# Output projection of a hybrid decoder trunk: a weight slice, three statistics steps and the softmax merge take other places in the order

## The reference

```python
h    = rms_norm(x) * (1 + scale) + shift             # scale, shift, gate = silu(c) @ w_ada + b_ada
proj = h @ w_in                                      # split among groups A, B, C
A = mla_attention(...)                               # prompt: causal; samples: 32 cached pages each
B = rwkv7_time_mix(...)                              # recurrence, then a norm over each head of 64:
      on = (o - mean(o)) * rsqrt(var(o) + 64e-5) * g + b + bonus
C = chunk_gmlp(...)
mixed = concat(silu(gA) * A, silu(gB) * B, silu(gC) * C)   # 1032 tokens x 1024
x = x + gate * rms_norm(mixed @ w_out)
```

## Time and profile before

| | us |
|---|---|
| median of 3 runs | 1941.46 |
| the profiled execution, its own time | 1939.73 |
| its span, first to last instruction | 1938.0 |
| PE busy in the span | 1833.1 |
| DVE busy | 894.3 |
| ACT busy | 512.0 |

### The profile page before, as it was taken

How to read it: one execution, slowest core, us unless ns; L and a number is a source line. 1 busy time by engine, 2 the same in 40 slices (tenths; PEclk the granted TensorE clock), 3 DMA queues, 4 the chain that set the end, 5 groups by cost and what they waited for, 6 DMA issues and landing times. The chain is left out here.

```text
span 1938.0 us, 45850 instructions
## 1 busy us (share of the span) xinstructions
PE 1833.1 (95%) x19344; PEld 1141.3 (59%) x19344; DVE 894.3 (46%) x1985; ACT 512.0 (26%) x1186; POOL 181.6 (9%) x175
## 2 busy tenths in 40 slices
PE   3999999999999899999969999999999989999998
PEld 2565666666665566654436656766666656666543
DVE  2125124223495678765230340332325857777642
ACT  3111122223331333432221110222224223343221
POOL 0010000002330300000000200000023321000000
PEclk9999999999999999999989999999999999999999
DMA  9600000000023666643155000010001147665441
GB/s 376 249 12 28 22 22 22 22 22 22 23 68 100 190 202 195 191 173 147 69 203 208 1 28 22 22 33 22 11 22 39 52 131 209 193 203 149 187 167 41
DMA packets 105543, 198.66 MB, mean 103 GB/s; under 512 B 17410, under 2 KB 87580, under 8 KB 101620
## 3 DMA queue, kind: packets, MB, share of 16 engines
q1 hardware_dynamic: 105332, 195.67, 30.6%
HBM read 182.81 MB, written 21.26 MB: 105 GB/s over the span
## 5 line engine op out<-in xcount | busy, mean ns | idle before, releaser
L825 PE MATMUL PB<-RB,R 128*128 128x344 f32 x1632 | 493.2, 455 | 0.0
L825 PEld LDWEIGHTS PB<-RB,R 128*128 128x128 f32 x1632 | 302.0, 190 | 156.4 <-issue 15.2
L1689 PE MATMUL PB<-WUQ,Q 32*32 32x256 f32 x5120 | 199.0, 385 | 20.1 <-DVE WUQ L1870 12.0
L2074 PE MATMUL PB<-RB,R 128*128 128x512 f32 x496 | 214.9, 593 | 0.0
L1870 DVE STREAM_TRANSPOSE WUQ<-RB 128x512 f32<-128x512 f32 x316 | 203.4, 680 | 17.8 <-DMA RB<-in_cache 14.2
L2074 PEld LDWEIGHTS PB<-RB,R 128*128 128x128 f32 x496 | 93.9, 190 | 115.9 <-issue 113.8
L985 ACT ACTIVATE R<-PB 128x344 f32<-128x344 f32 x90 | 41.3, 458 | 401.8 <-PE PB L825 401.8
L1240 DVE TENSOR_TENSOR PB<-PB,CST 128x128 f32<-128x128 f32 x64 | 18.8, 295 | 222.0 <-PE PB L845 222.0
L1689 PEld LDWEIGHTS PB<-WUQ,Q 32*32 32x32 f32 x5120 | 90.0, 104 | 43.9 <-issue 27.7
L673 PE MATMUL PB<-RB,R 128*128 128x344 f32 x288 | 85.4, 460 | 1.8 <-PEq L250 1.8
L1122 DVE COPY R<-PB 128x320 f32<-128x320 f32 x16 | 7.9, 492 | 146.7 <-PE PB L684 146.7
(11 more groups left out here) (367 smaller groups left out, 2617.5 us busy)
## 6 DMA issues: line engine op xcount, KB each, us to landing
RB<-in_cache SPq DMA_DIRECT2D x512, 160.0 KB, 2.6
R<-in_w_in SPq DMA_DIRECT2D x44, 512.0 KB, 3.8
R<-in_w_ada SPq DMA_DIRECT2D x14, 1536.0 KB, 9.7
RB<-in_w_ada SPq DMA_DIRECT2D x6, 1536.0 KB, 16.6
RB<-out_x_stream SPq DMA_DIRECT2D x2, 4096.0 KB
out_x_stream<-RB SPq DMA_DIRECT2D x16, 512.0 KB
RB<-in_x_prompt SPq DMA_DIRECT2D x1, 4096.0 KB
RB<-in_w_out SPq DMA_DIRECT2D x8, 512.0 KB, 3.8
```

The lines of the kernel that those rows point to most:

```text
L825: mm = pe.matmul(jobbank(j)[:, 0:CH], ring[:, blkno[n] % 4, k, :], hT[:, k, chunk(c)], start=(k == 0), stop=(k == KT - 1))
L1689: mm = pe.matmul(PB[qp[o], 2 * (h % 2) + q % 2, 0:256], Q4[qp[q], g, :], k[qp[q], c], start=(g == 0), stop=(g == NB - 1), skip_group_check ...
L2074: mm = pe.matmul(PB[0:n, 2 * (t % 2) + hf, :], mixT[:, k, cols(t)], wo[:, k, hf * 512:(hf + 1) * 512], start=(k == 0), stop=(k == 5))
```

## The change

`w_out` slice 2 is loaded at the end of the attention block instead of at the start of the output block, and a third `WP` multiplies by it. In the attention block's lists the items of the end are put in another order on PE and DVE, and `FC` uses PSUM bank 4 instead of 5 and waits for `pp_done` 16 (the copy of the last `PT`) instead of `ty_done` 8. In the output block `mean(4)`, `mean(5)`, `var(4)`, `var(5)` come earlier on PE, tile 2 is one call of `project`, `square(4)` and `square(5)` come ahead of `sums(0)` on ACT, and on DVE `centre(4)`, `centre(5)` and `leave(0)` come ahead of `finish(2)` and `finish(3)`.

```diff
-PE_PLAN = PE_PLAN[:4] + [(0, "GT", 0)] + PE_PLAN[4:-1] + [wp(0)] + rec("Z0") + PE_PLAN[-1:] + rec("U0") + [fc(1), (NH - 1, "PT", 0)] + \
-    rec("H0") + [fc(2)] + rec("Z1") + [pv(0), pv(1)] + rec("U1") + [pv(2), fc(4)] + rec("H1") + [pv(3)] + rec("OO") + [fc(6), wp(1)]
+PE_PLAN = PE_PLAN[:4] + [(0, "GT", 0)] + PE_PLAN[4:-1] + rec("Z0") + PE_PLAN[-1:] + [wp(0)] + rec("U0") + [(NH - 1, "PT", 0), fc(1)] + \
+    rec("H0") + [fc(2)] + rec("Z1") + [pv(0), pv(1)] + rec("U1") + [fc(4), pv(2), pv(3)] + rec("H1") + [wp(1)] + rec("OO") + [fc(6), wp(2)]
...
-DVE_PLAN = pair_plan(DVE_PAIR) + [fc(1), fc(2)] + rec("H0") + [fc(3)] + rec("G0") + [fc(4)] + rec("H1") + [fc(5), fc(6)]
+DVE_PLAN = pair_plan(DVE_PAIR) + [fc(1)] + rec("H0", "G0") + [fc(2), fc(3), fc(4)] + rec("H1") + [fc(5), fc(6)]
...
     sp.dma_start(wuv2, dram("w_uv")).then_inc(s_uv, 16)
+    sp.wait_ge(kt_used, NB * NH)
+    sp.dma_start(wo[:, 2], dram("w_out")[:, 2]).then_inc(s_wo[2], 16)
...
 elif what == "FC":
-    pe.wait_ge(ty_done, NS)
+    pe.wait_ge(pp_done, NH)
     if g == 1:
         pe.wait_ge(cb_done, 1)
-        pe.transpose(PB[0:1, 5, 0:P], m1, ident).then_inc(cb_full, 1)
+        pe.transpose(PB[0:1, 4, 0:P], m1, ident).then_inc(cb_full, 1)
...
-    for k in (2, 3):
-        sp.dma_start(wo[:, k], dram("w_out")[:, k]).then_inc(s_wo[k], 16)
+    sp.dma_start(wo[:, 3], dram("w_out")[:, 3]).then_inc(s_wo[3], 16)
...
-    project(0, [2, 3])
+    project(0, [3])
     var(2)
     var(3)
     project(0, [6, 7])
     project(1, [0, 1, 2, 3])
     project(0, [4, 5])
-    project(1, [6, 7, 4, 5])
     mean(4)
     mean(5)
-    project(2, [0, 1, 2, 3, 6, 7])
+    project(1, [6, 7])
     var(4)
     var(5)
-    project(2, [4, 5])
-    for t in ORD[3:]:
+    project(1, [4, 5])
+    for t in ORD[2:]:
...
     for u in (2, 3):
         root(u)
+    for u in (4, 5):
+        square(u)
     for i, t in enumerate(ORD):
...
         if i == 1:
-            for u in (4, 5):
-                square(u)
             for u in (4, 5):
                 root(u)
...
     variance(3)
+    centre(4)
+    centre(5)
+    leave(0)
     finish(2)
     finish(3)
-    leave(0)
     for i in range(1, 9):
...
         leave(ORD[i])
         if i == 1:
-            centre(4)
-            centre(5)
             variance(4)
```

More of the change, by code:

```diff
@@ L1728, in _ @@
                         elif what == "FC":
-                            pe.wait_ge(ty_done, NS)
+                            pe.wait_ge(pp_done, NH)
                             if g == 1:
                                 pe.wait_ge(cb_done, 1)
-                                pe.transpose(PB[0:1, 5, 0:P], m1, ident).then_inc(cb_full, 1)
+                                pe.transpose(PB[0:1, 4, 0:P], m1, ident).then_inc(cb_full, 1)
                             elif g == 2:
                                 pe.wait_ge(cb_done, 2)
-                                pe.matmul(PB[:, 5, 256:257], g128, ones[0:1, 0:1], start=True, stop=True, skip_group_check=True).then_inc(cb_full, 1)
+                                pe.matmul(PB[:, 4, 256:257], g128, ones[0:1, 0:1], start=True, stop=True, skip_group_check=True).then_inc(cb_full, 1)
                             elif g == 4:
@@ L1739, in _ @@
                                 pe.wait_ge(cb_done, 4)
-                                pe.matmul(PB[:, 5, 258:259], gsum, gl, start=True, stop=True, skip_group_check=True).then_inc(cb_full, 1)
+                                pe.matmul(PB[:, 4, 258:259], gsum, gl, start=True, stop=True, skip_group_check=True).then_inc(cb_full, 1)
                             elif g == 6:
@@ L1743, in _ @@
                                 for r in range(2):
-                                    mm = pe.matmul(PB[:, 5, r * 32:(r + 1) * 32], osb[:, r * P:(r + 1) * P], gsum[:, 0:32], start=True, stop=True, skip_group_check=True)
+                                    mm = pe.matmul(PB[:, 4, r * 32:(r + 1) * 32], osb[:, r * P:(r + 1) * P], gsum[:, 0:32], start=True, stop=True, skip_group_check=True)
                                 mm.then_inc(os_full, 1)
@@ L1956, in _ @@
                             dve.wait_ge(cb_full, 1)
-                            dve.tensor_reduce(gm1, PB[0:1, 5, 0:P].rearrange("p (c m) -> p m c", c=4), AX.X, ALU.max)
+                            dve.tensor_reduce(gm1, PB[0:1, 4, 0:P].rearrange("p (c m) -> p m c", c=4), AX.X, ALU.max)
                             dve.drain()
@@ L1961, in _ @@
                             dve.wait_ge(cb_full, 2)
-                            dve.tensor_scalar(nM, PB[:, 5, 256:257], -SCALE, None, ALU.mult).then_inc(cb_done, 1)
+                            dve.tensor_scalar(nM, PB[:, 4, 256:257], -SCALE, None, ALU.mult).then_inc(cb_done, 1)
                         elif what == "FC" and g == 4:
@@ L1974, in _ @@
                             dve.wait_ge(cb_full, 3)
-                            dve.reciprocal(rw, PB[:, 5, 258:259])
+                            dve.reciprocal(rw, PB[:, 4, 258:259])
                             dve.drain()
@@ L1988, in _ @@
                             dve.wait_ge(os_full, 1)
-                            dve.tensor_copy(olat[:].rearrange("p r h b -> p r b h"), PB[:, 5, 0:64].rearrange("p (r b h) -> p r b h", r=2, h=H))
+                            dve.tensor_copy(olat[:].rearrange("p r h b -> p r b h"), PB[:, 4, 0:64].rearrange("p (r b h) -> p r b h", r=2, h=H))
             pf_in = sem("pf_in")
```

## The result

The kernel after takes 1971.83 us (median of 4 runs, 1970.85 to 1985.81), the kernel before on the same chip 1944.09 (4 runs, 1939.73 to 1948.31). The ratio is 1.0152, interval 1.0128 to 1.0177: slower, as forecast. Times the 1941.46 that the prediction started from, that is +29.5 us to 1971.0, where 23.4 had been forecast, and the median is 0.8 us above the end of the range. The profiled execution took 1974.9 us, with a span of 1973.2.

A forecast was written before the change was run, and what follows sets the result against it. PE, busy 95% of the span, was taken as the bound. Per layer 2.8 (attention gaps) + 6.9 (tile 2) + 2.0 (half clock) = 11.7, twice 23.4: 1963.1 from the profiled execution, 1964.9 from the median, said 1964; range 1955 to 1971.

The forecast's parts named there:

- attention gaps, new less old: From the last scores to the output block: PE gaps of 4.4 us in, 1.6 out, +2.8 a layer.
- `WP` 2 in, slice out: `WP` 2 adds 1.9 us in the attention block, two `project` matmuls leave the output block, 1.7: nothing, or +0.2.
- tile 2's wait: Output block: PE stands still 6.9 us a layer at tile 2's first matmul, until DVE's `finish(3)` is over.
- half clock behind tile 2's wait: Output block: PE's work after the 6.9 us gap runs at half clock for a while, costing 2.0 us a layer.
- half clock in the tail: Between the scores' end and the output block: the three gaps of 1.0 to 1.7 us cost no half clock.
- The bound of the kernel: Whole kernel: PE bounds it, busy 95% of the span; idle time added there moves everything behind it.
- The end of the attention block: New PE gaps of 1.0 at `Z`, 1.7 at `FC` 1, 1.7 at `FC` 2; old 0.70, 0.36, 0.52 go.
- The output block: DVE idles 8 us before `mean(4)`, so `finish(3)` ends late and PE waits 6.9 us a layer at tile 2.
- B + 39.2: Output block, us counted from its start B: when DVE ends `finish(3)`; PE is free for tile 2 at B + 32.3.
- The moved slice and its load: `w_out` slice 2's early load lands in 3.8 us, long before `WP` 2: costs nothing; the moved work nothing, or +0.2.
- TensorE's clock: Half clock follows the 6.9 us gap at tile 2, 2.0 us a layer; the attention block's shorter gaps pay nothing.
- The rival that named the tail's half clock: Clock falls in the attention block's end too: another 1.7 us a layer, 1966.5, 1968 from the median; chance 0.15.

The follow-up runs named there:

- fill attention: Kernel after, with two unread matmuls of 384 columns on PE ahead of each of `FC` 1 and `FC` 2; ratio to before 1.0090.
- fill output: Kernel after, with seven unread matmuls of 512 columns on PE ahead of tile 2 in the output block; ratio to before 1.0131.
- Merge back: Kernel after with `FC` 1's place on PE, DVE's attention list, `FC`'s bank and wait as before, `WP` places kept; ratio to before 1.0081.
- finish first: Kernel after, with DVE's `finish(2)` and `finish(3)` put back ahead of `centre(4)`, `centre(5)` and `leave(0)`; ratio to before 1.0055.
- tile 2 split: Kernel after, with PE's `project` of tile 2 in two calls, slices 0 to 3, 6, 7, then 4, 5; ratio to before 1.0047.
- fill one gap: Kernel after, with two unread matmuls of 384 columns ahead of `FC` 1 alone; one execution, tails 19.85 and 21.23 us.

## Why the prediction was right in its direction and short in its size

Forecast and measurement of each term, both layers together. The tail without half clock is that of fill attention, 19.84 and 19.85, with 1.93 for `WP` 2 where it stands alone. The output block without it is before's, less the moved slice, plus the wait: 134.20 - 1.72 + 6.72 = 139.20, and 134.94 likewise; fill output's 139.03 and 135.14 agree within 0.2.

| term | forecast | measured | from |
|---|---|---|---|
| attention gaps, new less old | 5.6 | 5.2 | 2 x (19.85 - 15.30 - 1.93) |
| `WP` 2 in, slice out | 0 | 0.4 | 2 x (1.93 - 1.72) |
| tile 2's wait | 13.8 | 13.4 | the waits of PE |
| half clock behind tile 2's wait | 4.0 | 5.1 | (141.13 - 139.20) + (138.11 - 134.94) |
| half clock in the tail | 0 | 5.5 | (21.89 - 19.84) + (23.32 - 19.85) |
| sum | 23.4 | 29.7 | of the unrounded terms |

*The bound of the kernel*, PE without slack from tile 2 on: right. The delay of each stage came out whole at the end of its layer: 13.5 us in layer 1 and 16.2 in layer 2, where the forecast was 11.7 a layer.
*The end of the attention block*: right to 0.1 us in each of three gaps, in who ends them, and in the old gaps that went. Merge back shows that the merge steps' places and wait make the two of them ahead of `FC` 1 and 2.
*The output block*: right, down to DVE's idle time (8 forecast, 8.59) and B + 39.2 (39.1). One step on the way was misread: two `square` were put at 1.6, where the earlier trace rows has 1.07 for the two, and the 0.4 taken off for overlaps made up for most of it. That B + 39.2 is so near is in this part luck. That the order on DVE is the cause, and that the wait's place on PE is a second condition, finish first and tile 2 split show, each alone.
*The moved slice and its load*: neutral, as said; no wait of `WP` 2 for its load shows.
*TensorE's clock* is the step that failed. It was booked at 2.0 us a layer, at tile 2 alone, and the three gaps of the tail at nothing, because the earlier trace rows show gaps of 0.70 with the clock at full. But the earlier trace rows had already shown a gap of 1.93 that was enough, and the new ones are 0.97, 1.64 and 1.69. With them the clock did fall, and that cost 5.5 us in the two tails of after, where nothing was booked. In all 10 tails of the five traces with these gaps (after, its copy, finish first, tile 2 split, fill output) the clock fell, and the tail is longer than the 19.85 without half clock, by 1.3 to 4.2 us. In four of the ten (after and its copy) it fell behind the gap of 1.64 and before the one of 1.69, in the other six within the one of 1.69 or up to 0.4 us behind it. So it is not shown that it takes the sum of the two.

Nor does the length of a gap decide alone. The prediction called 1.93 the nearest shorter gap to 13.79, but the trace of before has gaps of 2.80, 2.57, 2.26 and 2.01 as well, and the one of 2.26 (to 1612.84) kept the clock. It also has a second gap of 1.93, behind matmuls of 344 columns, and the clock stayed at full (the row, and the window behind it):

```profile
572.36 1.42 PE L894 MATMUL PB<-RB,CST 128*128 128x344 f32 x4 [1.93 <-DVE R L1294]
...
572.00:575.00 3.00, 2.64 (x9) 1.81 (x10) 2.91 (x4) 0.00 (x0) 3.00 (x2) 1.00 0.03 5
```

The rival that named the tail's half clock had 0.15 and was itself too small: 1.7 a layer, where 2.0 and 3.5 were measured in after. What was held against it, that gaps of 0.70 leave the clock at full, is true of the trace of before and not of its copy (tail 2). With that rival the forecast would have been 1968, still 3 short; the rest is the 1.1 at tile 2 and the 2.1 by which the tail's half clock exceeds the rival's 3.4. Of the clock's return the prediction used one row, 4.6 us into the work. After the gaps of the kernel after it came back 5.0 and 8 us into the work in the tails, 4 and 6 at tile 2, layer 1 first each time.
The Trainium skill (TensorE: Matmul & The Clock Gate, "HAM oscillation") was drawn on for booking only the long wait. The trace does not agree with a reading by single long gaps: none in the tail exceeds 1.69 us, and in after half clock followed in both layers.
*The base.* The trace of before was of its fastest execution, 1939.73, and beside the experiments it took 1950.38 (median of 25) to 1956.82 (one run). The ratio is free of that, but a time in us is not: the forecast's range had 1 us for it.

## What to carry to other kernels

Price each new idle gap of a bounding PE twice, for its length and for the half clock that may follow it, and do so for gaps of 1.6 us too: here they were followed by half clock in all 10 tails that had two of them, and in one of two that had one. Before moving a step of an in-order engine behind a wait, look up when the waited-for engine gets there, and put a consumer's wait at the instruction that needs it, not at the head of its call. If a gap can't be closed, real work cut to its length is the best filling, and even unread matmuls shortened their stage here.

## What the runs showed of the hardware that was not expected

- Work that nobody reads made its stage faster: 4 matmuls in the tail took 2.0 and 3.5 us off it, 7 in the output block 2.1 and 3.0, by keeping the granted clock at 1.00.
- The same kernel at the same place, with the same gaps, can keep or lose the clock: 0.69 and 0.36 us in before (15.30 or 16.81 for the tail), one gap of 1.70 in fill one gap (19.85 or 21.23). Across places, a gap of 1.93 kept it at 572.36 and one of 1.93 lost it behind 610.98.
- The clock can fall after the gap is over: in the tails of after it fell 0.8 and 0.7 us into the work behind the gap of 1.64.
- The stretch outside the four stages scattered from 1643.3 to 1663.1 us over these traces, with no relation to the edits. One per cent between two single executions says nothing here.
